# A two-layer trunk in float32: the gates and the branch projections computed with tokens in the PSUM partitions instead of channels

## What is computed

```
h = rms_norm(x, norm_g[layer]) * (1.0 + scale) + shift
(qkv_a, z_a, beta_raw, alpha_raw, glu_in, z_b, q_c, k_c, v_c, z_c,
 q_i, k_i, w_i, gate_raw) = split_columns(h @ w_in[layer])
...
g_a, g_b, g_c = jnp.split(jax.nn.sigmoid(gate_raw + b_gate[layer]), 3, axis=-1)
merged = (g_a * (y_a @ w_proj_a[layer]) + g_b * (y_b @ w_proj_b[layer])
          + g_c * (y_c @ w_proj_c[layer]))
x = x + gate * (merged @ w_out[layer])
```

## Time and profile before

| | |
|---|---|
| median of 3 runs | 2540.09 us (2539.34 to 2546.92) |
| the profiled execution, its own time | 2543.15 us |
| its span, first to last instruction | 2541.4 us |
| PE busy | 2332.2 us, 92% of the span |
| POOL busy | 1688.8 us, 66% |
| DVE busy | 1220.3 us, 48% |
| ACT busy | 980.8 us, 39% |
| mean DMA rate | 186 GB/s |

### The profile page before, as it was taken

The page is one execution under the profiler, slowest core; times in us unless marked ns, Lnnn a source line. Parts: engine busy times, 40 slices in busy tenths (PEclk is TensorE's granted clock), DMA queues, the critical chain, the costliest instruction groups (busy, mean ns, idle before and its releaser), DMA issues.

```text
span 2541.4 us, 48278 instructions
## 1 busy us (share of the span) xinstructions
PE 2332.2 (92%) x18616; PEld 2279.7 (90%) x18616; DVE 1220.3 (48%) x1607; ACT 980.8 (39%) x1122; POOL 1688.8 (66%) x684
## 2 busy tenths in 40 slices
PE   4299999889999979999996999998899998999999
PEld 2299999879999979999996999998899998999999
DVE  6838744825553373434524683764545536421010
ACT  2033444373332434343423344435433334344442
POOL 0077858655554578888865776876555456888886
PEclk7599999999999999999997999999999999999999
DMA  9656646443333478888864564554333336876664
GB/s 397 261 166 179 207 127 179 129 140 108 116 116 107 126 250 295 285 296 281 316 222 148 161 202 141 171 167 127 112 113 119 112 102 214 282 251 178 182 211 162
DMA packets 212072, 473.63 MB, mean 186 GB/s; under 512 B 21184, under 2 KB 25408, under 8 KB 199264
## 3 DMA queue, kind: packets, MB, share of 16 engines
q1 hardware_dynamic: 211136, 469.48, 57.5%
q0 software_dynamic: 640, 2.10, 0.2%
q10 hardware_dynamic: 160, 0.13, 0.0%
HBM read 465.24 MB, written 6.29 MB: 186 GB/s over the span
## 4 chain that ended last, share of the span: by engine, by line
PE 68%; DVE 9%; POOL 8%; DMA 5%; ACT 4%; issue 3%; DVEq 2%; ACTq 0%; SPq 0%; POOLq 0%
PE ps L809 19%; PE ps L810 19%; PE ps L811 19%; POOL wl L475 8%; DVE acc L1211 2%; DMA raw<-w_out 2%; DMA raw<-w_pb 2%; DMA adaw<-w_ada 2%; PE ps L1034 1%; PE ps L1042 1%; ACT wh L498 1%; PE ps L1047 1%; DVE score L1350 1%; DVE ns L1517 1%; PE ps L870 1%
## 5 line engine op out<-in xcount | busy, mean ns | idle before, releaser
L475 POOL TENSOR_TENSOR wl<-raw,wh 128x1024 fp32r<-128x1024 f32 x672 | 1684.1, 2506 | 791.8 <-ACT wh L498 710.4
L809 PE MATMUL ps<-ah,wh 128*128 128x256 f32 x4544 | 1315.2, 289 | 70.4 <-POOL wl L475 37.4
L810 PE MATMUL ps<-al,wh 128*128 128x256 f32 x4544 | 1296.5, 285 | 0.0
L811 PE MATMUL ps<-ah,wl 128*128 128x256 f32 x4544 | 1296.0, 285 | 0.0
L498 ACT CAST wh<-raw 128x1024 fp32r<-128x1024 f32 x672 | 701.1, 1049 | 1262.8 <-PE ps L811 1009.5
L809 PEld LDWEIGHTS ps<-ah,wh 128*128 128x128 f32 x4544 | 883.7, 194 | 79.6 <-POOL wl L475 32.0
L810 PEld LDWEIGHTS ps<-al,wh 128*128 128x128 f32 x4544 | 883.8, 194 | 3.6 <-issue 3.3
L811 PEld LDWEIGHTS ps<-ah,wl 128*128 128x128 f32 x4544 | 882.5, 194 | 0.0
L809 PE MATMUL ps<-yh,wh 128*128 128x256 f32 x768 | 222.0, 289 | 6.9 <-POOL wl L475 6.9
L811 PE MATMUL ps<-yh,wl 128*128 128x256 f32 x768 | 217.2, 283 | 0.0
L810 PE MATMUL ps<-yl,wh 128*128 128x256 f32 x768 | 217.1, 283 | 0.0
(11 more groups left out here) (245 smaller groups left out, 1824.7 us busy)
## 6 DMA issues: line engine op xcount, KB each, us to landing
raw<-w_in SPq DMA_DIRECT2D x512, 512.0 KB, 3.6
modw<-w_ada SPq DMA_DIRECT2D x64, 1024.0 KB, 6.9
adaw<-w_ada SPq DMA_DIRECT2D x32, 1024.0 KB, 7.5
raw<-w_out SPq DMA_DIRECT2D x64, 512.0 KB, 4.8
raw<-w_pc SPq DMA_DIRECT2D x32, 512.0 KB, 3.7
raw<-w_pb SPq DMA_DIRECT2D x32, 512.0 KB, 4.5
raw<-w_pa SPq DMA_DIRECT2D x32, 512.0 KB, 3.9
xs<-xt SPq DMA_DIRECT2D x2, 2048.0 KB, 10.6
```

What stands on the lines that cost most here:

```text
L475: nc.gpsimd.tensor_tensor(wl[:, s], raw[:, s], wh[:, s].bitcast(F32), ALU.subtract).then_inc(sem("w_split"), 1)
L809: M.matmul(o, lh, rh, start=start, stop=False, skip_group_check=True)
L810: M.matmul(o, lh, rr, start=False, stop=False, skip_group_check=True)
L811: return M.matmul(o, ll, rh, start=False, stop=last, skip_group_check=True)
```

## The change

Only turns c, b and a change, and what hangs on them.

- `gemm(..., tok=True)`: the activations are the stationary operand (two tiles of 128 tokens), and the weights move, 512 columns at a time. A round is 2 row tiles x 2 token tiles x 3 = 12 matmuls. The result has tokens in the partitions.
- `b_gate` now lies along the columns: it is loaded over all partitions by a DMA of 256 KB per turn into `gbias` (on SP, between g7 and p0) and added by DVE in PSUM (`gate_add`), which ACT's tanh waits for (`gate_sum`). In b and a turns `gate_add` stands between units 1 and 2 on DVE; in c turns behind inverse level 3. The tanh is one instruction of 128x1024 instead of four of 128x256.
- `merged` is kept by token (`mtok`), and PE transposes it, 8 transposes of 128x128 for each quarter: three quarters in the projection of a3 ahead of row tiles 1, 3 and 5, the last in wout0 ahead of row tile 4 (`turn_merged`). The first waits for a3's `gate_tanh`, since it overwrites PSUM pair 0. ACT and DVE read the transposed quarters from PSUM.
- `mod_sum(GATING)` moves into the gate of b3, and `mod_sum(SHIFT)` into that of a3, both ahead of row tile 10 (g5). On DVE, `mods_from(SHIFT)`, which waits for the latter, moves from behind a3 to ahead of it.
- SP's loop over turns is unrolled.

```diff
-                with sp.Fori(0, 3) as i:
-                    turn(i, False)
-                turn(3, True)
+                        sp.wait_ge(sem("gbias_free"), i + (12 * layer + 4 * "cba".index(br) + 1))
+                        sp.dma_start(gbias[:], b_gate[layer:layer + 1, bass.ds(i * GW + GATE[br] * D, GW)
+                                                      ].broadcast_to([P, GW])).then_inc(sem("gbias_landed"), 16)
                         group(wp[br], i * GW, i * TURN + (hc + G_IN), G_PR, unit=unit2)
...
-                def gate_tanh(i, br, at, n):
-                    act.wait_ge(sem("w_used"), i * TURN + (at + G_IN))
+                def gate_tanh(i, n):
+                    act.wait_ge(sem("gate_sum"), i + (n + 1))
                     act.wait_ge(sem("gate_free"), i + (n + 1))
-                    for ct in range(4):
-                        last = A.activation(gate[:, ct], ps[:, ct // 2, (ct % 2) * T:(ct % 2 + 1) * T], ACT.Tanh,
-                                            bias=hbg[:, bass.ds(i * 4 + (GATE[br] * KT + ct), 1)], scale=0.5)
-                    last.then_inc(sem("gate_ready"), 1)
+                    tanh_half(gate[:], ps[:, 0:2, :]).then_inc(sem("gate_ready"), 1)
...
+                for q in range(G_PR):
+                    rounds(hc + 3 * TURN + G_IN + q, 1, q)
+                    if q < 3:
+                        merged_high(q)
...
-                        for ct in range(4):
+                        for tt in range(TT if tok else 0):
+                            t = slice(tt * P, (tt + 1) * P)
+                            mm = three(ps[:, 2 * pair + tt, :], (mv[0][:, t], mv[1][:, t]),
+                                       (wh[:, s, k], wl[:, s, k]), kt == n * HK - 1, kt == 0)
+                        for ct in range(0 if tok else 4):
...
+                def turn_merged(q):
+                    if q == 0:
+                        pe.wait_ge(gemm_free[0], gn[0] + 5)
+                    if q == 1 and layer < DEPTH - 1:
+                        pe.wait_ge(sem("shift_taken"), 1)
+                    pe.wait_ge(sem("merge_done"), 12 * layer + 9 + q)
+                    for ct in range(4):
+                        for tt in range(TT):
+                            at = (ct % 2) * T + tt * P
+                            mm = M.transpose(ps[:, MERGED_B[q] + ct // 2, at:at + P],
+                                             mtok[:, tt, q * GW + ct * P:q * GW + (ct + 1) * P], ident)
+                    mm.then_inc(sem("merged_turned"), 1)
...
+                def gate_add(i, at, n):
+                    dve.wait_ge(sem("gbias_landed"), (i + (n + 1)) * 16)
+                    dve.wait_ge(sem("w_used"), i * TURN + (at + G_IN))
+                    V.tensor_tensor(ps[:, 0:2, :], ps[:, 0:2, :], spread(gbias[:], 1, [P, TT, GW]), ALU.add
+                                    ).then_inc(sem("gate_sum"), 1)
+                    done("gbias_free")
...
-                turn_mods(3, "a", True)
+                if not last_layer:
+                    dve.wait_ge(sem("mod_summed"), 3 * layer + 4)
+                    mods_from(layer + 1, SHIFT).then_inc(sem("shift_taken"), 1)
+                turn(3, "a", 12 * layer + 8)
```

More of the change, by code:

```diff
@@ L125, in bucket_rows, with trunk @@
     return hot
-def trunk(nc, xt, cvec, rel_bias, w_ada, w_in, w_pa, w_pb, w_pc, w_out, params, consts, hot, out):
+def trunk(nc, xt, cvec, rel_bias, w_ada, w_in, w_pa, w_pb, w_pc, w_out, b_gate, params, consts, hot, out):
     ctx = ExitStack()
@@ L1133, in _, with gating_sum, shift_sum @@
+                def gating_sum():
+                    pe.wait_ge(sem("mod_used"), 2 + passes[0] + KT)
+                    mod_sum(GATING, 0)
+                def shift_sum():
+                    pe.wait_ge(sem("mod_used"), 2 + passes[1] + KT)
+                    mod_sum(SHIFT, 1)
+                gate_turns(2, 0, 3)
+                gate_turns(2, 3, 1, before={MOD_T: [gating_sum]})
                 hc += 4 * TURN
                 gn = [gn[0] + 4, gn[1] + 4]
-                pe.wait_ge(sem("mod_used"), 2 + passes[0] + KT)
@@ L1136, in _ @@
-                pe.wait_ge(sem("o_rms"), L1)
-                mod_sum(GATING, 0)
-                with pe.Fori(0, 4) as i:
-                    gemm(i * TURN + hc, i + gn[0], 0, H)
-                    pe.wait_ge(sem("y_split"), 3 * layer + 3)
-                    gemm(i * TURN + (hc + G_IN), i + gn[1], 1, Y, G_PR)
+                def turn_merged(q):
[10 more added lines that the diff above has]
+                    mm.then_inc(sem("merged_turned"), 1)
@@ L1142, in _ @@
+                gate_turns(3, 0, 3)
+                gate_turns(3, 3, 1, before={MOD_T: [shift_sum]} if layer < DEPTH - 1 else None,
+                           before_proj={2 * q + 1: [lambda q=q: turn_merged(q)] for q in range(3)})
                 hc += 4 * TURN
                 gn = [gn[0] + 4, gn[1] + 4]
-                if layer < DEPTH - 1:
-                    pe.wait_ge(sem("mod_used"), 2 + passes[1] + KT)
-                    mod_sum(SHIFT, 1)
-                group(0, H, quarter=("merged_split", 4 * layer))
+                group(0, H, quarter=("merged_split", 4 * layer),
+                      before={MERGED_T: [lambda: turn_merged(3)]})
@@ L1238, in _ @@
                 passes = mod_units(layer)
-                if layer > 0:
-                    V.tensor_scalar(hbg[:], p_(layer, "b_gate"), 0.5, None, ALU.mult)
                 dve.wait_ge(sem("mod_summed"), 3 * layer + 2)
@@ L1642, in _, with turn @@
                 V.scalar_tensor_tensor(qg, qg, 0.5, zs[0][:], ALU.mult, ALU.mult).then_inc(sem("ya_ready"), 1)
-                def turn_mods(i, br, last):
-                    plan = turn_units(layer, br, last)
+                def turn(i, br, n0):
+                    plan = turn_units(layer, br, i == 3)
                     if plan:
@@ L1648, in turn_mods @@
                         at = passes[(part + 1) % 3] + kt
-                        k0 = 0 if last else i * 4
-                        if last:
+                        k0 = 0 if i == 3 else i * 4
+                        if i == 3:
                             V.memset(acc[:, 1 - part], 0.0)
-                        for n in range(4):
+                    for n in range(4):
+                        if n == 2:
+                            gate_add(i, hc, n0)
+                        if plan:
                             mod_unit(k0 + (kt + n), k0 + (at + n), n % 2, 0 if part == GATING else 1 - part)
-                for i in range(3):
-                    turn_mods(i, "b", False)
+                for i in range(4):
+                    turn(i, "b", 12 * layer + 4)
                     merge(i, hc, 12 * layer + 4, False)
-                turn_mods(3, "b", True)
-                merge(3, hc, 12 * layer + 4, False)
                 hc += 4 * TURN
@@ L1684, in _ @@
                 hc += 4 * TURN
-                if not last_layer:
-                    dve.wait_ge(sem("mod_summed"), 3 * layer + 4)
-                    mods_from(layer + 1, SHIFT)
                 dve.wait_ge(sem("x_landed"), 16 * (L1 + 1))
```

80 lines of the change are left out of this document (46 added, 34 removed).

## The result

The changed kernel takes 2558.44 us (median of 4 runs, 2554.64 to 2563.6), the kernel before, run beside it, 2540.19 us (4 runs): ratio 1.0072, 95% interval 1.0058 to 1.0087. It is slower by 18 us, 0.7%. The profiled execution took 2556.64 us, its span 2554.9 us against 2541.4 us before.

A forecast was written before the change was run, and what follows sets the result against it. PE was taken as the bound in layer 1's b and a and part of c, POOL and DMA in layer 0's b and a; -7.8 - 2.2 - 1.9 + 12 = +0.1 us gave 2540 us, range 2523 to 2558.

The forecast's parts named there:

- The price X: Duration of one 512-column matmul on PE: taken as 0.228 us, making a round 2.74 us, 0.14 less.
- Rivals A: Weight loading on PE hidden entirely, a 512-column matmul at 0.216 us: total 2524 us; chance 0.17.
- B: Rival: the excess per matmul grows with the columns, 0.238 to 0.240 us each: slower, 2555 us; chance 0.28.
- fixed excess gives 0.226: Model of a 512-column matmul: 0.213 us for the columns plus the same 0.013 us as at 256 columns.
- Rounds 0 to 4 of a c turn are DVE's, 5 to 11 are PE's: c turns, both layers: PE waits for DVE's preparation in the first rounds; only the later seven are PE-bound.
- 8 turns x 7 PE-bound rounds x 0.14 = -7.8 us: c turns, both layers: saving of 0.14 us in each PE-bound round, -7.8 us in all.
- stands where DVE waits: c turns: the bias addition, 1.22 us on DVE, falls where DVE waits for PE's next `inv_x` anyway.
- b and a of layer 0 at 0: Layer 0's b and a turns hang on POOL and DMA, so a faster PE waits there: 0 us.
- b and a of layer 1: Layer 1: b -2.2 us; a -1.9 us, from -6.7 for rounds, +3.5 for transposes and +1.3 waiting for tanh.
- a3 and w_out of layer 0: Late shift-row copy delays loads and tanh, PE idles 10 us, unit 4 comes later: +12 us, bounds +8 to +15.
- the 12 stay: Layer 0's wout0 to wout3 are POOL's and DMA's already, so the +12 us delay is not recovered.
- Rival C: The stall in layer 0's a3 does not form, its end costs some 3 us: total 2531 us; chance 0.08.

The follow-up runs named there:

- 1: Changed kernel with weights moved 256 columns at a time in the c turns alone: 2544.0 us, ratio to before 1.0009.
- 2: Changed kernel with POOL's subtraction in the c turns cut to 32 columns per row tile, so not the whole computation: 2517.67 us, one run.
- 3: Kernel before with POOL's subtraction in the c turns cut to 32 columns per row tile, so not the whole computation: 2518.94 us, one run.
- 9: Also written `e10_split_after`: changed kernel with POOL's subtraction in the c turns issued as four pieces: 2523.63 us, ratio to before 0.9918.
- 10: Also written `e11_split_before`: kernel before with POOL's subtraction in the c turns issued as four pieces: 2530.51 us, ratio 0.9955.
- 6: Kernel before with ACT's three exponentials ahead of its second weight rounding in the c turns: 2559.36 us, one run; before 2538.03 beside it.
- e5_exps_after: Changed kernel with ACT's three exponentials ahead of its second weight rounding in the c turns: 2558.07 us, ratio 1.0073.
- e12_split_mods_late: Changed kernel with the c turns' subtraction in four pieces and DVE's shift-row copy later in layer 0's a3: 2519.99 us, ratio 0.9915.
- 4: Changed kernel with DVE's copy of the shift rows moved later in a3 of layer 0, behind its second unit: 2554.5 us, ratio 1.0044.

## Why the prediction was wrong, and where right

- **The price X was right.** 0.226 to 0.227 us against 0.228. Rivals A and B both hung on another X and both fall. B's total, 2555 us, came near the measured 2558 by luck: its matmul of 0.238 to 0.240 us is not there. The sentence "fixed excess gives 0.226" was the right model: 0.013 us a matmul at 256 columns as at 512.
- **The step that failed** is "Rounds 0 to 4 of a c turn are DVE's, 5 to 11 are PE's", and "8 turns x 7 PE-bound rounds x 0.14 = -7.8 us" with it. It took DVE's chain for one of fixed length that a faster PE cannot touch. PE's rounds free the weight slots, so they set when ACT rounds and when POOL subtracts, and POOL's subtraction sets how long DVE's operations take: 0.69 or 2.87 us. Measured: +14.2 us. The earlier trace rows held the sign of it, a `ns` of 2.12 us that should take 0.69 (it ends 0.55 us behind POOL's subtraction of 694.85), and I read it only as part of the wait. I had used the collision once, for POOL (4.15 us in place of 2.41), and did not ask for DVE. Shown by 1 (columns alone bring it back), 2 and 3 (without the subtraction it is gone), 9 and 10 (with all the work, shorter pieces, it is nearly gone), 6 (it can be brought into the kernel before).
- **The bias addition "stands where DVE waits"**: right; 1 keeps it and loses nothing.
- **b and a of layer 0 at 0** were mis-sized: -4.7 from b0 to a3. `mod_sum`'s place of its own (3.49 us) is gone, and b0 takes 37.7 us in place of 40.4. b1 and b2 stay at the 34.6 forecast (34.9 and 34.1). That PE draws on POOL's lead in b0 is an argument, not shown.
- **Ahead of b0**, +1.2 and +1.3 us were not forecast at all (the last rounds before b0 took 35.5 in place of 34.2 us); in other traces it is absent in the changed kernel (34.3 and 34.4 us in `e5_exps_after`) and present in the kernel before (35.2 and 35.1 in `e11_split_before`). So it is not the wide form's own; its cause is open.
- **b and a of layer 1**: -4.0 and -4.4 where -2.2 and -1.9 stood. 48 rounds gained 0.16 and not 0.14; the half-clock stretch behind the 32 passes, 1.5 us in a0 before, is now inside b3; transposes and the wait for tanh cost 4.9, as forecast (4.8).
- **a3 and w_out of layer 0**: the stall of 10 us came as described (9.8), and so did the later unit 4. The sum, 12, was near (10.1), by two errors. w_out's first part ended 15.4 us later relative to a3's start, 3.2 of them because a3's gate part ended later than forecast (above). And 5.3 us are missing again in wout1 to wout3, so "the 12 stay" was wrong for these two traces. But 4.4 of the 5.3 lie in wout3 (40.0 us before, 35.6 after), and wout3 takes anything from 32.8 to 39.8 us in the other traces, 39.8 in `e10_split_after` and 33.2 in `e12_split_mods_late`. With one trace of each kernel, this can be spread; that 10.1 came near 12 is luck in part. Rival C is refuted.

The error of the sum: c turns 22 us too low, all the rest together 8 us too high; 13.7 in place of 0.1. The measured medians lie another 5 us apart.

What stays open: what sets the length of layer 0's wout3, how the end of layer 0 could be kept at its old length (4 shows that moving one wait is not enough), and the 1.2 us ahead of b0. The light subtractions (2 and 3) and the exponentials in the kernel before (6) are single runs.

## What to carry to other kernels

Before a wait for an engine is priced, look whether its operations take their own time: the same instruction at two durations (0.69 and 2.1 or 2.9 us) was a collision here, and its price hangs on who starts first by tenths of a microsecond. An edit that shifts either engine can then cost more than it saves, and is tested fairly only with the collision made cheap. Cutting the blocking engine's operation into pieces does that where that engine has slack; the round's length beside the time of the pieces tells where it has.

## What the runs showed of the hardware

- A blocked DVE operation takes the rest of POOL's operation plus 0.55 us (0.69 alone, so it overlaps the last 0.14); when DVE is first, POOL's takes 0.42 longer.
- Four POOL subtractions of 256 elements a partition take 2.83 us, one of 1024 takes 2.40: 0.14 us for each further piece, and 0.24 more between rounds either way.
- PE's waits of 0.62, 1.50 and 0.98 us in c2 were followed by 3.5 us with a granted clock of 0.52; in c1 waits of 0.62, 1.50 and 0.99 us were not (1.00 throughout). 32 one-column passes (3.6 us, PE busy throughout) were followed by a granted clock of 0.57 in the changed kernel's b3 of layer 0.
